# Value projections and one query tile interleaved with the first row scores of three attentions

## The reference

```python
# first block: differential attention (4 heads, 2 maps each) and windowed attention with sinks
# ("mix"), 16 meta tokens ahead of both, gated merge, SwiGLU
h = h + mixer_block(rms_norm(h, norm_mix[layer]), w_in[layer], ...)
h = h + swiglu(rms_norm(h, norm_ffn[layer]), ...)
# second block, layer 0: short convolution and latent attention ("mla")
q = (rms_norm_2(c_q, q_norm) @ w_q_up)      # 8 heads, 64 + 32 rotated
kv = (rms_norm_2(c_kv, kv_norm) @ w_kv_up)  # keys 64, values 64
y_mla = dense_causal_attention(q, k, v)
# second block, layer 1: compressed, selected and windowed attention ("nsa"), 16 heads
out = gate0 * o_cmp + gate1 * o_slc + gate2 * o_win
# each layer: x = x + rms_norm_2(sq_relu_mlp(h, w1, w2), g)
```

## Time and profile before

| | us |
|---|---|
| median of 3 runs (2139.6 to 2141.73) | 2140.38 |
| the profiled execution | 2139.3 |
| its span, first to last instruction | 2137.5 |
| TensorE busy in the span | 2046.3 |
| VectorE busy | 1188.1 |
| ScalarE busy | 810.8 |
| mean granted clock of TensorE, of 1 | 0.977 |

### The profile page before, as it was taken

How to read it: one execution, slowest core, us unless ns; L and a number is a source line. 1 busy time by engine, 2 the same in 40 slices (tenths; PEclk the granted TensorE clock), 3 DMA queues, 4 the chain that set the end, 5 groups by cost and what they waited for, 6 DMA issues and landing times. The chain is left out here.

```text
span 2137.5 us, 27608 instructions
## 1 busy us (share of the span) xinstructions
PE 2046.3 (96%) x10766; PEld 971.4 (45%) x10766; DVE 1188.1 (56%) x2179; ACT 810.8 (38%) x1476; POOL 38.5 (2%) x40
## 2 busy tenths in 40 slices
PE   7979999999999999989999999999879999999997
PEld 3434444444444444444444444447434444444443
DVE  5956744546554347666576623267476645865222
ACT  3437732324222232346333322235167742432220
POOL 2000000000000002000000000000000000000000
PEclk9989999999999999999999999997989999999998
DMA  5300133324333322312233333316000031533311
GB/s 200 108 1 1 50 94 96 107 62 138 106 99 109 104 74 89 99 49 76 64 110 108 102 112 101 99 58 215 26 1 1 11 99 30 155 101 102 108 48 40
DMA packets 52185, 179.19 MB, mean 84 GB/s; under 512 B 5984, under 2 KB 9696, under 8 KB 51680
## 3 DMA queue, kind: packets, MB, share of 16 engines
q1 hardware_dynamic: 52064, 177.51, 27.1%
HBM read 174.34 MB, written 2.10 MB: 83 GB/s over the span
## 5 line engine op out<-in xcount | busy, mean ns | idle before, releaser
L1677 DVE SCALAR_TENSOR_TENSOR w_lo<-w_raw,w_hi 128x1024 f16<-128x1024 f32 x317 | 385.6, 1220 | 172.4 <-ACT w_hi L1338 159.7
L1338 ACT ACTIVATE w_hi<-w_raw 128x1024 f16<-128x1024 f32 x317 | 330.9, 1049 | 279.0 <-PE pS L931 271.9
L929 PE MATMUL pS<-arena,w_hi 128*128 128x512 f16 x924 | 350.9, 380 | 4.6 <-DVE w_lo L1677 3.1
L929 PE MATMUL pS<-xx,w_hi 128*128 128x512 f16 x928 | 352.9, 380 | 1.4 <-DVE xx L1692 1.4
L930 PE MATMUL pS<-xx,w_hi 128*128 128x512 f16 x928 | 353.1, 381 | 0.0
L931 PE MATMUL pS<-xx,w_lo 128*128 128x512 f16 x928 | 352.9, 380 | 0.0
L930 PE MATMUL pS<-arena,w_hi 128*128 128x512 f16 x924 | 350.9, 380 | 0.0
L931 PE MATMUL pS<-arena,w_lo 128*128 128x512 f16 x924 | 350.7, 380 | 0.0
L1347 ACT ACTIVATE arena<-src 128x512 f16<-128x512 f32 x106 | 66.7, 629 | 321.3 <-DVE src L2279 164.0
L1748 DVE TENSOR_TENSOR tmp<-pS,rs 128x512 f32<-128x512 f32 x98 | 67.5, 689 | 137.9 <-PE pS L931 137.9
L929 PEld LDWEIGHTS pS<-arena,w_hi 128*128 128x128 f16 x924 | 91.0, 98 | 114.4 <-DVE w_lo L1677 3.6
(11 more groups left out here) (333 smaller groups left out, 2680.4 us busy)
## 6 DMA issues: line engine op xcount, KB each, us to landing
w_raw<-in_w SPq DMA_DIRECT2D x317, 512.0 KB, 3.6
X<-in_x SPq DMA_DIRECT2D x1, 2112.0 KB, 8.1
arena<-in_c SPq DMA_DIRECT2D x2, 1024.0 KB, 6.8
out_t<-X SPq DMA_DIRECT2D x8, 256.0 KB, 2.0
arena<-in_h SPq DMA_DIRECT2D x4, 256.0 KB, 14.2
arena<-in_h SPq DMA_DIRECT2D x2, 512.0 KB, 10.0
arena<-in_c SPq DMA_DIRECT2D x2, 256.0 KB, 2.8
arena<-arena SPq DMA_DIRECT2D x4, 128.0 KB, 2.5
```

Of the source, the lines that this page charges most:

```text
L929: pe.matmul(ps, wh, ah, start=f, stop=False)
L1338: act.activation(w_hi[:, u % WR, :], w_raw[:, u % RAW, :], ACT.Copy, scale=WS).then_inc(hi_split, 1)
L1677: dve.scalar_tensor_tensor(out=w_lo[:, u % WR, :], in0=w_raw[:, u % RAW, :], scalar=WS, in1=w_hi[:, u % WR, :], op0=ALU.mult, op1=ALU.subt ...
```

## The change

- Order of stages: kb goes ahead of va; vm goes behind qn; ck2, cv2 and gt go ahead of vv. A stage of kind "N" that needs alignment may now skip tiles over a unit's end (two are skipped ahead of vv).
- Banks: va, vb, vm and vv take banks 0 to 2 in turn; ck2 and cv2 have banks 4 and 5. kb's meta part goes to pT, va's to pO bank 0, vb's to pO bank 1.
- `attention` takes a function `beside` that is called behind each chunk of row scores in the steps with s < 0 (on TensorE behind the meta scores too). In mix it makes va tiles 1 to 3 in pieces of two k (six matmuls) and vb in whole tiles; in mla qn tile 3 in pieces and vm; in nsa vv, but for its first piece, in pieces of two k. VectorE's function evicts each tile behind a row maximum that comes later; ScalarE's writes the halves of qn 3.
- The first key scores of each attention wait for the last value eviction.
- `stop` is set to the next value in step 0 instead of at the start of an attention, and is rounded up to whole units (`whole_units`).
- The last four copies of rotated query rows count on a semaphore of their own, `rope_last`.

```diff
@@ class Plan, bank choice
+                elif s.name in HOME:
+                    b = HOME[s.name]
+                elif s.name in INSIDE:
+                    b = (INSIDE[s.name] + j) % 3
@@ STAGES
-    [("qa", ...), ("qb", ...), ("ka", ...), ("va", "N", NQ, KD, 4),
-     ("kb", "T", 1, KD, 1), ("vb", "N", NQ, KD, 1)]
+    [("qa", ...), ("qb", ...), ("ka", ...), ("kb", "T", 1, KD, 1),
+     ("va", "N", NQ, KD, 4), ("vb", "N", NQ, KD, 1)]
-       ... ("qr", "T", 2, 6, 1), ("vm", "N", NQ, 2, 4), ("qn", "T", 4, 6, 1),
+       ... ("qr", "T", 2, 6, 1), ("qn", "T", 4, 6, 1), ("vm", "N", NQ, 2, 4),
-       ("q2", "T", 8, KD, 1), ("vv", "N", NQ, KD, 4),
-       ("ck2", "T", 1, 1, 1), ("cv2", "T", 1, 1, 1), ("gt", "N", NQ, KD, 1),
+       ("q2", "T", 8, KD, 1), ("ck2", "T", 1, 1, 1), ("cv2", "T", 1, 1, 1), ("gt", "N", NQ, KD, 1),
+       ("vv", "N", NQ, KD, 4),
+def whole_units(name):
+    return -(-PL.st[name].tau0 // TPU) * TPU
@@ TensorE
             def key_scores(t, i):
+                if u == RUNS["mix"].u0:
+                    pe.wait_ge(evicted, S["vb"].o0 + NQ)
                 if u == RUNS["mla"].u0:
-                    pe.wait_ge(evicted, S["qn"].o0 + NQ)
+                    pe.wait_ge(evicted, S["vm"].o0 + NQ)
+                if u == RUNS["nsa"].u0:
+                    pe.wait_ge(evicted, S["vv"].o0 + NQ)
+            def values_mix(x):
+                if x == 0:
+                    pe.wait_ge(rhs_ready, PL.r["kb"] + 1)
+                if x < 12:
+                    tile_N(S["va"], full, 1 + x // 4, x % 4 * 2, x % 4 * 2 + 2)
+                elif x < 16:
+                    tile_N(S["vb"], full, x - 12, 0, KD, pO[0:M, 1, 0:P] if x == 12 else None)
+            def rest_mla(x):
+                if x in (0, 2, 3):
+                    tile_T(S["qn"], 3, of(cqs), (0, 0, 2, 4)[x], (2, 2, 4, 6)[x])
+                if x == 11:
+                    pe.wait_ge(rope_last, 16 * 4)
+                if x in (5, 6, 8, 9):
+                    tile_N(S["vm"], lambda q, k: cks[q][:, k, :], {5: 0, 6: 1, 8: 2, 9: 3}[x], 0, 2)
+            def values_nsa(x):
+                if x + 1 < 16:
+                    tile_N(S["vv"], full, (x + 1) // 4, (x + 1) % 4 * 2, (x + 1) % 4 * 2 + 2)
-            def attention(run):
+            def attention(run, beside=None):
                 for kind, n, c in run.pre:
                     extra_scores(kind, n, c)
+                    beside(x)
+                    x += 1
...
                             nat_scores(nxt, i)
+                            if s < 0 and beside is not None:
+                                beside(x)
+                                x += 1
...
-            out_N(S["va"], full, meta=pT[0:M, 1, :])
-            out_T(S["kb"], 0, xr, meta=(pO[:, 1, 0:M], xm))
+            out_T(S["kb"], 0, xr, meta=(pT[:, 1, 0:M], xm))
             pe.wait_ge(evicted, S["qb"].o0 + 2)
-            out_N(S["vb"], full, meta=pO[0:M, 0, 0:P])
+            tile_N(S["va"], full, 0, 0, KD, pO[0:M, 0, :])
...
-            pe.wait_ge(rope_laid, 16 * 12)
+            pe.wait_ge(rope_laid, 16 * 8)
...
             out_N(S["gt"], full)
+            tile_N(S["vv"], full, 0, 0, 2)
@@ VectorE
+            def values_mix(g):
+                if g in (2, 6, 10):
+                    value_a((g + 2) // 4)
+                elif 11 <= g < 15:
+                    value_b(g - 11)
+            def values_nsa(g):
+                if g in (3, 7, 11):
+                    value_c((g + 1) // 4)
+            def rest_mla(g):
+                if g == 4:
+                    ... evict qn 3
+                if g == 6:
+                    ... low halves of qn 3
+                if g in (7, 8, 9, 10):
+                    value_m(g - 7)
```

More of the change, by code:

```diff
@@ L70 @@
 SPARE = ("ks", "qb")
+HOME = {"ck2": 4, "cv2": 5}
+INSIDE = {"va": 0, "vb": NQ, "vm": 0, "vv": 0}
 class Stage:
@@ L933, in out_T, with tile_T @@
                         mm.then_inc(mm_done, 1)
+            def tile_T(s, j, rhs, k0, k1):
+                o = s.o0 + j
+                if k0 == 0:
+                    bank_free(o)
+                for k in range(k0, k1):
+                    tau = s.tile(j, k)
+                    wh, wl = weights(tau)
+                    pe.matmul(out_bank(o), wh, rhs(0, k), start=k == 0, stop=False)
+                    pe.matmul(out_bank(o), wh, rhs(1, k), start=False, stop=False)
+                    mm = pe.matmul(out_bank(o), wl, rhs(0, k), start=False, stop=k == s.k - 1)
+                    if (tau, 0) in PL.marks:
+                        mm.then_inc(mm_done, 1)
@@ L935, in out_N, with tile_N @@
             def out_N(s, lhs, meta=None):
+                for t in range(NQ):
+                    tile_N(s, lhs, t, 0, s.k, meta if t == 0 else None)
+            def tile_N(s, lhs, t, k0, k1, meta=None):
                 w = s.width * P
-                for t in range(NQ):
+                if k0 == 0:
                     bank_free(s.o0 + t)
[L940 to L954, removed]
@@ new lines, in tile_N @@
+                ps = out_bank(s.o0 + t)[:, 0:w]
+                a = slice(t * P, (t + 1) * P)
+                for k in range(k0, k1):
+                    tau = s.tile(0, k)
+                    wh, wl = weights(tau, s.width)
+                    f, l = k == 0, k == s.k - 1
+                    if meta is not None:
+                        pe.matmul(meta, lhs(0, k)[:, T:TM], wh, start=f, stop=False)
+                        pe.matmul(meta, lhs(0, k)[:, T:TM], wl, start=False, stop=False)
+                        pe.matmul(meta, lhs(1, k)[:, T:TM], wh, start=False, stop=l)
+                    pe.matmul(ps, lhs(0, k)[:, a], wh, start=f, stop=False)
+                    pe.matmul(ps, lhs(0, k)[:, a], wl, start=False, stop=False)
+                    mm = pe.matmul(ps, lhs(1, k)[:, a], wh, start=False, stop=l)
+                    if (tau, t) in PL.marks:
+                        mm.then_inc(mm_done, 1)
@@ L1475, in attention @@
                             pending = nxt.c + i
+                            g += 1
+                            if run.slots[0].kind.name == "mla" and g == 6:
+                                head_parts("qn", 3, lambda half: qm[:, 0, 6 + half, :])
+                                for n in range(NQ):
+                                    out_of(S["vm"], n)
                         e = run.ended(s - 2)
@@ L1576, in _ @@
                 out_of(S["qr"], j)
-            for t in range(NQ):
-                out_of(S["vm"], t)
             out_of(S["qn"], 0)
@@ L1638, in _ @@
                 out_of(S["gt"], j)
+            for t in range(NQ):
+                out_of(S["vv"], t)
             act.preload_act_table_set("natural_log_exp_and_others")
@@ L1992, in attention @@
+            def attention(run, dst, look_tau, stop_tau, beside=None):
+                g = 0
                 for n, (kind, qi, c) in enumerate(run.pre):
                     extra_max(kind, qi, n, c)
+                if run.slots[0].kind.name == "nsa":
+                    value_c(0)
                 for n, (kind, qi, c) in enumerate(run.pre):
@@ L2010, in attention @@
                             nat_max(nxt, i)
+                            if s < 0 and beside is not None:
+                                beside(g)
+                                g += 1
                         now = run.unit(s, i)
```

129 lines of the change are left out of this document (69 added, 60 removed).

## The result

The changed kernel took 2106.03 us (median of 4 runs, 2105.47 to 2108.59) beside 2141.06 us (2139.6 to 2142.33) for the kernel before on the same chip: a ratio of 0.9839, 95% interval 0.9822 to 0.9856, 35 us less. Run again later on another occasion it was 2106.24 us, ratio 0.984 (0.9826 to 0.9853). The span of the profiled execution fell from 2137.5 to 2103.7 us, by 33.8; the sum gave 35.2 before I took 6.5 off for the clock.

The account below looks back on a forecast made before the run. TensorE was taken to bound the kernel, idling in the three openings; gains of 9.3 + 7.8 + 18.1 = 35.2 us, less 6.5 for the clock, gave 28.7, so 2112 us, range 2101 to 2125.

Parts of the forecast that it names:

- the sum: The three openings' gains at the upper clock level, 9.3 + 7.8 + 18.1 = 35.2 us, before the clock deduction.
- The bound: Whole kernel: TensorE's records fill 96% of the span; only stretches where it waits or runs at the lower clock can give.
- First opening: First attention, row scores before first key scores: key scores at 152.0, 9.3 us sooner, evictions hidden under TensorE's pieces.
- The six microseconds of evictions: First opening: three va and four vb evictions on VectorE, 6 us, hide under TensorE's pieces.
- Second opening: Second attention: VectorE binds; first maximum at 940.9, key scores at 959.6 against 967.37, 7.8 us sooner.
- the walk: Step-by-step timing of each attention's opening up to its first key scores, at the upper clock; gains sum to 35.2 us.
- Third opening: Third attention: first maximum at 1536.0, key scores at 1559.1, 18.1 us sooner; the 5.9 us wait is included.
- The clock: Low-level spells in the sparse starts of the openings: 2.5, 1 and 3 us taken off, 6.5 in all.
- (B): Rival: TensorE stays at the lower clock level in the openings; 17 us slower, 2157; chance 0.06.
- (C): Rival: pieces lengthen the round trip, only the w_lo waits' 9.0 us go, 2131; chance 0.12 including times up to the forecast.
- (D): Rival: clock stays up throughout, key scores no longer start at half level; 38 us gained, 2102; chance 0.12.

Follow-up runs that it names:

- e1: Changed kernel with only the first attention's pieces undone, va tiles 1 to 3 and vb projected in one block ahead of the row scores; 2117.2 us, ratio 0.9894.
- e2: Changed kernel with only the second attention's pieces undone, qn tile 3 and all of vm projected ahead of the row scores; 2107.09 us, ratio 0.9849.
- e4: Kernel before with only the limits on splitting ahead rounded up to whole units behind the second and third attention; 2130.18 us, ratio 0.9954.
- e3: Changed kernel with only the third attention's pieces undone, vv projected in one block ahead of meta and row scores; 2121.5 us, ratio 0.9915.
- e11: Changed kernel with 16 unread matmuls added early in the first attention, 8 ahead of the first piece and 8 behind the second; 2105.84 us, ratio 0.9838.
- e6: Changed kernel with 38 unread matmuls added early in the first attention, 8 ahead of the first piece and 30 behind the second; 2110.89 us, ratio 0.9861.
- e7: Changed kernel with 26 unread matmuls added, two behind each chunk without a piece in the first and third attention; 2105.33 us, ratio 0.9833.
- e0: The changed kernel itself, run again on a later occasion; 2106.24 us, ratio 0.984 to the kernel before.
- e5: Changed kernel with va tiles 2 and 3 each projected in one piece of 24 matmuls (5.2 us) instead of four of six; 2110.49 us, ratio 0.9857.
- e10: Changed kernel with first and third attention's pieces placed earlier and further apart, plus unread matmuls behind the third opening's last chunks; 2096.82 us, ratio 0.9791.

## Why the prediction was right

**The bound** held: where TensorE had waited for the round trip, it now works, and the gain ends with the third opening. Behind it, before and after take 560.31 and 560.38 us to the end.

**First opening**, step by step: first maximum predicted 117.2, measured 117.33; ninth chunk behind it, at which the pieces of va end, 133.2 and 133.16; end of vb 143.4 and 143.66; key scores 152.0 and 151.87. The price of a chunk with a piece, 1.8 us, was 1.78. The six microseconds of evictions hid under the pieces as said. Since e1 gives all of it back, this was right for its reason too.

**Second opening**: 6.9 at the key scores where the walk had 7.8. Right in size, but in part for the wrong reason. TensorE reached the row scores 3.2 us later than predicted (929.49 + 9.42 = 938.9, against 935.7), because the rope rows come sooner and VectorE waits for them (3.07 us for the rope's matmuls, L1297); the 5.2 us for the halves of three q tiles had in part been done meanwhile, so that the first maximum is only 1.5 late (942.4 against 940.9). I had written that VectorE binds there, and didn't draw the conclusion that the pieces then bring nothing; nor did my expectation for e2. The runs give 3.7 for the unit limit (e4) and 0.35 for the pieces (e2). The other 2.8, vm behind qn so that VectorE starts on q sooner, is what remains and was not run by itself.

**Third opening**: first maximum predicted 1536.0, measured 1520.13 + 16.31 = 1536.4; key scores 1559.1 and 1559.6; 17.6 instead of 18.1. e3 shows that it rests on the pieces in this order, and e4 that 7.5 of it could have been had without.

**The clock** is the step that failed, a term of the sum mis-sized: 6.5 us taken off, of which the traces show 0 to 1. The sum of the walk, 35.2, was within 1.4 of the measured 33.8. Of what is missing, 0.9 lies in the second opening, where the level was 1.00, and 0.5 in the third. That the time still fell well inside the range is owed to the walk and to a wide range, not to this term. The level did fall where I said that it would, in the sparse start (0.50 from 107 to 116), and came back when the pieces ran without a break. But I had added up the spells without asking who binds there. Ahead of the first maximum it is VectorE (8.4 of 9 us busy), and e11 shows that TensorE's level there moves nothing. In the second opening there was no spell at all (1.00). In the third, the runs differ by some 0.8 us between 1500 and 1512: e1, e6 and e7 lose that much against e0 there, and e2 and e5 don't. What a level of 1.00 in that stretch would give to the changed kernel as it stands was not run.

**The rivals.** (B) would have shown pieces at 0.43 us in the long run; they have 0.216 at a level of 1.00. The Trainium skill, "TensorE: Matmul & The Clock Gate", section "A second HAM failure mode: psum-queue depth-cycling", would let the level swing while TensorE cycles through banks; by it the 2157 of (B) would have come out, and the openings don't bear it out. The stretch from 118.9 to 145.9 cycles through five banks at 1.00, though with waits of only 1.1 us in 27; the one from 1520.1 to 1543.3 has waits of 4.1 in 23.2 us and a level of 0.99, the one from 929.4 to 951 waits of 3.6 in 21.6 and 1.00. (C): the pieces didn't lengthen the round trip at 1.3 us each, and do at 5.2 (e5); its 9 us for the waits alone came near e4's 9.8 to 11. (D) was right that the clock costs almost nothing on the way to the key scores, but not that it stays up (0.50 from 107 to 116, 0.76 from 1505 to 1512), and it expected key scores at the upper level; they are at 0.69 and 0.66. With that put right by e7 the first attention gives nothing and the third 1.5 us.

## What to carry to other kernels

Work of the bound engine that is moved into a stretch where it waits can hide there in pieces shorter than the round trip (1.3 us against 2.26 here; 5.2 did not hide, and nothing between was run). The gain is not the work moved but the waits that it fills: 23.7 us of va and vb moved into the first opening brought 9.4, for then TensorE itself sets the pace. And it is next to nothing (0.35 us in the second) where another engine is fuller: ask for each opening which engine is full, and expect its gain from there alone. A low clock level is to be charged only where TensorE sets the next event. And a limit that is rounded down to a unit can cost more than the wait that it shows, for what stands behind the wait is then done one by one (5.89 us of wait, 7.0 of delay).

## What was not expected of the hardware

The same code of the sparse start has shown quite different levels in different runs, with no difference behind it: between 107 and 111 us 0.50 in the changed kernel and e0, 0.57 in e5, 0.64 in e7; the first maximum, offsets off, is 117.0 in all four. The very first matmuls of the kernel keep a spacing of 0.43 us until 16.6 in e0 and until 19.1 in e7, from the same start at 14.07, and this moves the whole execution by 1.3 us. A spell near 1700 that some executions have (e0) and others don't (e3, e10) moves it by 1.7 us. Both are as much as some of the effects looked for here; only the comparison of the same instruction in two traces separates them. At the first key scores of the third attention, the upper level is worth 1.5 us over 4.7 us of work; at those of the first, nothing.
